# One mask product ahead of each group of attention scores, in a kernel of two transformer blocks

## The chip, the cores and the metric

The kernel runs on one core of a Trainium2 chip. The metric is the device time of one execution in microseconds. TensorE (PE) multiplies and writes to PSUM; VectorE (DVE) and ScalarE (ACT) read PSUM and do the elementwise work; GpSimd (POOL) does a few small operations; SyncE (SP) issues the weight transfers.

## The reference

The input is 256 positions of width 1024. Two blocks follow each other. The first has a causal softmax attention with a forgetting term (8 heads of 64), a retention branch, an output projection and an MLP, all modulated by a small vector c. The second applies a sparse attention (8 heads of 64 in two key groups) with pooling, an MLP, gated linear attention and another MLP, with layer norms between. For the change only the scores and their mask matter. First attention:

```python
logits = einsum(q, k) * scale
logits = logits + cum[:, :, s0:s1, None] - cum[:, :, None, :s1]
logits = where(q_pos >= k_pos, logits, -inf)
p = softmax(logits)
```

The second attention has three branches. The compressed branch scores 15 summary keys. The selected and the window branch see, at 256 positions (16 selected blocks are more than there are, and the window is 512), all keys up to the query, so each is a causal softmax over the same q with its own keys and values:

```python
s_s = einsum(q, k_sel);  p_s = masked_softmax(s_s, kpos <= t)
s_w = einsum(q, k_w);    p_w = masked_softmax(s_w, wmask)
o = gates[0] * o_c + gates[1] * o_s + gates[2] * o_w
```

## The kernel before

All matrices with weights are streamed. SyncE fetches tiles of 128 x 1024 fp32 into 6 slots, ScalarE rounds each to its high part (`whi`, L581) and VectorE takes the low part (`wlo`, L1107), and PE multiplies in three products, high by high, high by low and low by high (`three`, L1766 to L1768 and L1906 to L1908). Each engine runs a program in an order written out by hand. Semaphores are counted up by one engine and waited for by another.

Both attentions are woven into the projections around them. The dictionaries `between` name, behind which weight tile, which steps of the attention PE does. A step `S_(n)` computes the scores of group n, `T_(n)` transposes its probabilities, `V_(n)` multiplies them with the values. The groups (`GRP`, `GROUPS`) are the same in three branches: the first attention (n = 0 to 5), the selected branch (6 to 11) and the window branch (12 to 17). In each, two groups hold four heads of the first query tile (t = 0, 128 keys each) and four groups hold two heads of the second (t = 1, 256 keys each). Either way a group fills one PSUM bank of 512 fp32 columns.

`softmax_scores(n)` issues the scores. It first waits until ScalarE has taken the exponentials of the group that had the same bank (`at_exp`). Then for each head it multiplies q (stationary, 128 queries wide) with k (streamed, `kw` = 128 or 256 columns), in fp32 (L1989), which the trace shows as two passes with a weight load each. In the first attention q and k have 104 rows (64 of the head, and rows that carry the forgetting sums); in the second they have 64. Behind each head's product stands the mask product (L1990): the identity as stationary operand, `negb` streamed, both bf16 128 x 128. `negb` is 0 where a key is allowed and -1e30 where it lies ahead of the query. It is added to the head's last 128 columns, the diagonal block. Both are cast once, at the start (L725, L726). The last mask product of the group counts `at_mm` up.

Then VectorE takes each head's maximum (`maxima`, L1339), ScalarE the exponentials with their sums (`exps`, L804), VectorE in the second attention scales them by gate over sum (`weigh`, L1571 to L1575, counts `at_w`). `prob_transposes` (L2002) waits for these, VectorE copies the result out (L1347), and the values follow (L2094, L2304, L2308). The compressed branch's own scores (`cmp_scores`, L2252) are 64-row products of 15 columns, right behind `S_(6)`. The pooling products (L2321, L2322, L2330) stand between groups 11, 12 and 13.

As this kernel uses PSUM, a product with `start=True` opens a bank: it overwrites where it writes, and a product with `start=False` adds where something has been written since the bank was opened and overwrites elsewhere. The MLP (`up`) relies on this already: it opens the bank with the first product only and writes the other half with `start=False`.

Of the kernel before, what the change touches and what calls it, by code (L numbers as in the profile page):

```python
# [12 lines left out]
P = 128  # L13
# [155 lines left out]
def block_program(nc, dram, out):  # L169
    with ExitStack() as ctx:  # L170
        def sb(name, shape, dt=F32):
            return ctx.enter_context(nc.sbuf_tensor(name, shape, dt))
# [12 lines left out]
        rows = sb("rows", [P, 2, D])  # L185
        proj = sb("proj", [P, NT, 3072])
        qT = sb("qT", [P, 2 * D])
        kT = sb("kT", [P, 2 * D])
# [7 lines left out]
        identb = sb("identb", [P, P], BF16)  # L196
        negb = sb("negb", [P, P], BF16)
# [26 lines left out]
        AT = ctx.enter_context(nc.psum_tensor("AT", [P, 4, 512], F32))  # L224
# [58 lines left out]
        def bank(pb, t):  # L283

            if pb == 2:
                return AT[:, 2 + t, :]
            return PJ[:, 2 * (1 - pb if pb < 2 else pb % 2) + t, :]
# [25 lines left out]
        S_BANK = [0, 1, 0, 1, 0, 1] + [1] * 12  # L313
# [1433 lines left out]
        def _(pe):  # L1747
            mm = nc.tensor.matmul
# [21 lines left out]
            def tile_part(o, s, t, hi, lo, k0, n=512, start=False, stop=False):  # L1770

                for kk in range(KPT):
                    w = slice(512 * kk, 512 * kk + n)
                    ins = three(o[:, 0:n], hi[:, k0 + kk, rows_of(t)], lo[:, k0 + kk, rows_of(t)], whi[:, s % SPL, w],
                                wlo[:, s % SPL, w], start and kk == 0, stop and kk == KPT - 1)
                return ins
# [199 lines left out]
            def softmax_scores(n):  # L1976

                br, t, heads = GROUPS[n]
                fox = n < NF
                before = [g for g in range(0 if fox else NF, n) if S_BANK[g] == S_BANK[n]]  # L1980
                if before:
                    pe.wait_ge(at_exp, before[-1] + 1)
                kw = P * (t + 1)
                for u, h in enumerate(heads):
                    rows = slice(0, 104) if fox else slice(0, 64)
                    q = qT[rows, h * S + t * P:h * S + (t + 1) * P]
                    k0 = h * S if fox else (1024, 1536)[br] + S * (h // 4)
                    o = AT[:, S_BANK[n], u * kw:(u + 1) * kw]
                    mm(o, q, kT[rows, k0:k0 + kw], start=True, stop=False)  # L1989
                    ins = mm(o[:, kw - P:kw], identb[:, :], negb[:, :], start=False, stop=True)  # L1990
                ins.then_inc(at_mm, 1)

            def prob_transposes(n):
# [79 lines left out]
            def fox_scores(n):  # L2073
                if n == 2:
                    pe.wait_ge(hd_done, 8)
                if n == 0:
                    pe.wait_ge(hd_done, 4)
                    pe.wait_ge(cum_done, 2)
                    pe.wait_ge(ld_sel, 32)
                    pe.wait_ge(cast_done, 3)  # L2080
                softmax_scores(n)
# [87 lines left out]
            for q in range(4):  # L2169
                pe.wait_ge(xn_done, q // 2 + 1)  # L2170
                for c in range(4):
                    ins = nc.tensor.transpose(PJ[:, q, c * P:(c + 1) * P], from_proj(q // 2, 4 * (q % 2) + c), ident)
                ins.then_inc(xt_tr, 1)
            mod_sums(0)
            for s, (b, i) in enumerate(FIRST):
                for t in range(NT):
# [6 lines left out]
                    ins = tile_part(bank(b, t), T_IN + s, t, hT_hi, hT_lo, KPT * i, 512, i == 0, i == BLK - 1)  # L2183
# [97 lines left out]
            def nsa_scores(n):  # L2281
                if n == NF:
                    pe.wait_ge(nt_done, 7)
                softmax_scores(n)
# [215 lines left out]
```

## Time and profile before

| | |
|---|---|
| median of 3 runs | 1027.58 us (1026.83 to 1028.77) |
| profiled execution | 1029.0 us, of which the span is 1027.2 us |
| PE busy | 966.0 us, 94% of the span |
| VectorE, ScalarE busy | 657.4 us, 485.8 us |
| mean granted clock of PE | 0.984 |
| DMA, mean | 182 GB/s |

Times in the rows are microseconds from the start of the span, unless marked ns. PE's matmul records overlap, since products are pipelined: the distance between two starts tells what a product costs the stream behind it, its own length also contains its way through the array. PEld is the weight load, which usually runs beside the product before it. "x2" joins neighbouring instructions of one line. PEclk is the clock granted to PE as a share of 2.4 GHz. The first attention's scores lie between 84 and 117 us, the second's between 422 and 500 us; the MLPs are the long stretches between.

### The profile page before, as it was taken

The page shows a single profiled execution, that of the slowest core. Times are in us where ns is not written, and L with a number is a line of the kernel's source. Part 1 is how long each engine was busy: PE and PEld are TensorE (multiplying, and loading weights), DVE is VectorE, ACT ScalarE, POOL GpSimd, SP SyncE. Part 2 cuts the span into 40 slices and gives each one's busy share as a digit, 9 for nine tenths or more (in the row PEclk, how much of TensorE's full clock was granted, in tenths as well). Part 3 has the DMA queues.
Part 4 walks back from the last instruction along what each step waited for, and adds up shares of the span by engine and source line. Part 5 has one row for each costly group of instructions (what it writes and reads, how often), then busy time and mean ns, then how long its engine had stood idle before and what let it go on. Part 6 is the DMA issues. An engine that isn't in the chain of part 4 may idle for free.

```text
span 1027.2 us, 14930 instructions
## 1 busy us (share of the span) xinstructions
PE 966.0 (94%) x5602; PEld 824.2 (80%) x5602; DVE 657.4 (64%) x828; ACT 485.8 (47%) x734; POOL 54.0 (5%) x59
## 2 busy tenths in 40 slices
PE   3889989799999999999989999998999989999996
PEld 3768867599999987866679999996786779999995
DVE  5777897885455666555876546548545786555555
ACT  5457657454454444333345445443645725544440
POOL 3030101100000001000020000001000010000000
PEclk9999989999999999899999999999999999999998
DMA  9999776686655666411447655663542357456531
GB/s 281 297 240 290 206 210 230 234 272 206 205 178 172 209 232 159 124 41 43 143 131 237 201 199 163 196 206 106 181 150 84 118 170 263 167 187 203 183 123 41
DMA packets 109991, 186.94 MB, mean 182 GB/s; under 512 B 8696, under 2 KB 67088, under 8 KB 109920
## 3 DMA queue, kind: packets, MB, share of 16 engines
q1 hardware_dynamic: 104800, 177.33, 53.8%
q0 software_dynamic: 2592, 8.53, 3.0%
q8 instruction: 34, 0.56, 0.2%
q10 hardware_dynamic: 2544, 0.35, 0.2%
q14 instruction: 21, 0.17, 0.0%
HBM read 185.13 MB, written 1.05 MB: 181 GB/s over the span
## 4 chain that ended last, share of the span: by engine, by line
PE 81%; DVE 8%; ACT 4%; issue 3%; DMA 2%; POOL 2%; SPq 0%; POOLq 0%; ACTq 0%; DVEq 0%
PE PJ L1766 14%; PE PJ L1767 14%; PE PJ L1768 14%; PE AT L1908 8%; PE AT L1907 8%; PE AT L1906 8%; PE AT L1989 2%; POOL rstd L467 2%; DVE wlo L1107 1%; PE AT L2002 1%; PE AT L1757 1%; DMA raw<-in_w_out_dram 1%; PE AT L2033 1%; DMA raw<-in_w_in_dram 1%; DVE bn L1192 1%
## 5 line engine op out<-in xcount | busy, mean ns | idle before, releaser
L1107 DVE TENSOR_TENSOR wlo<-raw,whi 128x1024 fp32r<-128x1024 f32 x144 | 172.9, 1222 | 53.0 <-ACT whi L581 52.5
L1906 PE MATMUL AT<-hT_hi,whi 128*128 128x256 f32 x720 | 203.8, 283 | 0.0
L1908 PE MATMUL AT<-hT_hi,wlo 128*128 128x256 f32 x720 | 203.8, 283 | 0.0
L1907 PE MATMUL AT<-hT_lo,whi 128*128 128x256 f32 x720 | 203.7, 283 | 0.0
L1235 DVE TENSOR_TENSOR wlo<-raw,whi 128x1024 fp32r<-128x1024 f32 x144 | 169.9, 1222 | 32.2 <-ACT whi L639 31.6
L1766 PE MATMUL PJ<-whi,uhi 128*128 128x512 f32 x432 | 170.9, 396 | 1.5 <-DVE wlo L1107 0.9
L581 ACT ACTIVATE whi<-raw 128x1024 fp32r<-128x1024 f32 x144 | 146.9, 1055 | 48.7 <-DMA raw<-in_w_in_dram 28.5
L1767 PE MATMUL PJ<-wlo,uhi 128*128 128x512 f32 x432 | 169.4, 392 | 0.0
L1768 PE MATMUL PJ<-whi,ulo 128*128 128x512 f32 x432 | 168.7, 391 | 0.0
L639 ACT ACTIVATE whi<-raw 128x1024 fp32r<-128x1024 f32 x144 | 144.5, 1051 | 47.6 <-PE PJ L1768 43.7
L1766 PE MATMUL PJ<-whi,hT_hi 128*128 128x512 f32 (+1 forms) x320 | 133.0, 416 | 11.4 <-DVE hT_lo L1283 7.3
L1907 PEld LDWEIGHTS AT<-hT_lo,whi 128*128 128x128 f32 x720 | 138.0, 192 | 1.7
L1906 PEld LDWEIGHTS AT<-hT_hi,whi 128*128 128x128 f32 x720 | 138.0, 192 | 1.6
L1908 PEld LDWEIGHTS AT<-hT_hi,wlo 128*128 128x128 f32 x720 | 138.0, 192 | 0.0
L1244 DVE TENSOR_TENSOR pr<-pr 128x512 f32<-128x512 f32 x45 | 31.1, 692 | 161.6 <-ACT pr L649 161.6
L1768 PE MATMUL PJ<-whi,hT_lo 128*128 128x512 f32 (+1 forms) x320 | 126.0, 394 | 0.0
L1767 PE MATMUL PJ<-wlo,hT_hi 128*128 128x512 f32 (+1 forms) x320 | 125.9, 393 | 0.0
L649 ACT ACTIVATE pr<-AT 128x512 f32<-128x512 f32 x45 | 26.9, 598 | 190.3 <-PE AT L1908 190.3
L1766 PEld LDWEIGHTS PJ<-whi,uhi 128*128 128x128 f32 x432 | 81.6, 189 | 18.8 <-issue 1.9
L1768 PEld LDWEIGHTS PJ<-whi,ulo 128*128 128x128 f32 x432 | 81.5, 189 | 17.5
L1767 PEld LDWEIGHTS PJ<-wlo,uhi 128*128 128x128 f32 x432 | 81.7, 189 | 15.3 <-issue 0.2
L1766 PEld LDWEIGHTS PJ<-whi,hT_hi 128*128 128x128 f32 x320 | 62.2, 194 | 29.2 <-DVE hT_lo L1283 8.7
(310 smaller groups left out, 1079.5 us busy)
## 6 DMA issues: line engine op xcount, KB each, us to landing
raw<-in_mlp_w_dram SPq DMA_DIRECT2D x128, 512.0 KB, 4.8
raw<-in_w_in_dram SPq DMA_DIRECT2D x32, 512.0 KB, 6.1
raw<-in_w_ada_dram SPq DMA_DIRECT2D x32, 512.0 KB, 5.1
raw<-in_w_mlp_in_dram SPq DMA_DIRECT2D x32, 512.0 KB, 4.9
raw<-in_w_mlp_out_dram SPq DMA_DIRECT2D x32, 512.0 KB, 5.0
raw<-in_c_w_in_dram SPq DMA_DIRECT2D x24, 512.0 KB, 4.5
raw<-in_w_ada_dram SPq DMA_DIRECT2D x32, 256.0 KB, 5.9
raw<-in_a_w_in_dram SPq DMA_DIRECT2D x12, 512.0 KB, 5.4
```

Of the source, the lines that this page charges most:

```text
L581: nc.scalar.activation(whi[:, s % SPL, :], raw_slot(r), ACT.Copy).then_inc(hi_done, 1)
L639: nc.scalar.activation(whi[:, s % SPL, :], raw_slot(r), ACT.Copy).then_inc(hi_done, 1)
L649: nc.scalar.activation(pr[:, 0, :], AT[:, j % 2, :], ACT.Relu).then_inc(relu_done, 1)
L1107: tt(wlo[:, n % SPL, :], raw_slot(r), whi[:, n % SPL, :].bitcast(F32), ALU.subtract).then_inc(raw_done, 1)
L1235: tt(wlo[:, s % SPL, :], raw_slot(r), whi[:, s % SPL, :].bitcast(F32), ALU.subtract)\
L1244: tt(pr[:, 1, :], pr[:, 0, :], pr[:, 0, :], ALU.mult).then_inc(usq, 1)
L1766: mm(o, a, hi, start=start, stop=False)
L1767: mm(o, a, lo, start=False, stop=False)
L1768: return mm(o, b, hi, start=False, stop=stop)
L1906: mm(o, whi[:, s % SPL, c], hT_hi[:, k, :], start=first, stop=False, skip_group_check=True)
L1907: mm(o, whi[:, s % SPL, c], hT_lo[:, k, :], start=False, stop=False, skip_group_check=True)
L1908: ins = mm(o, wlo[:, s % SPL, c], hT_hi[:, k, :], start=False, stop=last, skip_group_check=True)
```

## The change

The mask product moves from behind each head's scores to the head of the group, and there is one for all heads. Its output is the last 128 of each head's `kw` columns: for t = 0 the whole bank, for t = 1 two runs of 128 columns with 128 between them. Its streamed operand is `negb`, repeated for each head by a stride of zero. It opens the bank (`start=True`). The score products then have `start=False`: they add to the mask in the diagonal blocks and overwrite in the first 128 columns of t = 1. The last score product of the group counts `at_mm` up.

```diff
--- before.py
+++ after.py
@@ -1981,13 +1981,15 @@
                 if before:
                     pe.wait_ge(at_exp, before[-1] + 1)
                 kw = P * (t + 1)
+                n_heads = len(heads)
+                mm(AT[:, S_BANK[n], :].rearrange("p (u k) -> p u k", u=n_heads)[:, :, kw - P:kw], identb[:, :],
+                   negb[:, :].unsqueeze(1).broadcast_to([P, n_heads, P]), start=True, stop=False, skip_group_check=True)
                 for u, h in enumerate(heads):
                     rows = slice(0, 104) if fox else slice(0, 64)
                     q = qT[rows, h * S + t * P:h * S + (t + 1) * P]
                     k0 = h * S if fox else (1024, 1536)[br] + S * (h // 4)
                     o = AT[:, S_BANK[n], u * kw:(u + 1) * kw]
-                    mm(o, q, kT[rows, k0:k0 + kw], start=True, stop=False)
-                    ins = mm(o[:, kw - P:kw], identb[:, :], negb[:, :], start=False, stop=True)
+                    ins = mm(o, q, kT[rows, k0:k0 + kw], start=False, stop=True, skip_group_check=True)
                 ins.then_inc(at_mm, 1)
 
             def prob_transposes(n):
```

## Rows read from the trace of the kernel before

**Rows 1.** The page, chain that ended last: share of the span by engine.

```profile
PE 81%; DVE 8%; ACT 4%; issue 3%; DMA 2%; POOL 2%; SPq 0%; POOLq 0%; ACTq 0%; DVEq 0%
```

**Rows 2.** Windows: start:end us, length, busy us of each engine (instructions), PEclk, DMA share, GB/s.

```profile
458.00:468.00 10.00, 10.00 (x63) 7.38 (x62) 7.13 (x14) 6.00 (x14) 0.00 (x0) 1.00 0.33 105
...
500.00:512.00 12.00, 9.57 (x60) 6.90 (x60) 10.96 (x19) 5.40 (x9) 0.00 (x0) 1.00 0.55 175
...
535.00:600.00 65.00, 64.93 (x412) 58.98 (x412) 40.49 (x40) 33.49 (x39) 0.00 (x0) 1.00 0.63 207
```

**Rows 3.** The score products, PE: ns min/median/max, first and last start, forms.

```profile
L1989 PE MATMUL AT<-kT,qT x96: 272/376/579, 84.4 to 498.7; 64*128 64x128 f32 x32, 64*128 64x256 f32 x32, 104*128 104x128 f32 x16, 104*128 104x256 f32 x16
```

**Rows 4.** PE timeline, four heads, 104 rows: start us, us, engine, line, operands, count [idle <-releaser].

```profile
84.67 0.22 PE L1990 MATMUL AT<-negb,identb 128*128 128x128 bf16 x1
84.73 0.44 PE L1989 MATMUL AT<-kT,qT 104*128 104x128 f32 x2
85.00 0.22 PE L1990 MATMUL AT<-negb,identb 128*128 128x128 bf16 x1
```

**Rows 5.** PE timeline, two heads, 104 rows, first group on the chain.

```profile
95.54 0.60 PE L1989 MATMUL AT<-kT,qT 104*128 104x256 f32 x2
95.98 0.22 PE L1990 MATMUL AT<-negb,identb 128*128 128x128 bf16 x1
...
96.55 0.47 PE L1766 MATMUL PJ<-whi,hT_hi 128*128 128x512 f32 x1
```

**Rows 6.** Timeline of PE's weight loads (PEld), compressed branch's scores, 64 rows.

```profile
425.17 2.42 PEld L2252 LDWEIGHTS AT<-sc,qT 64*128 64x128 f32 x21
```

**Rows 7.** PE timeline, four heads, 64 rows, full clock.

```profile
467.53 0.48 PE L1989 MATMUL AT<-kT,qT 64*128 64x128 f32 x2
467.95 0.23 PE L1990 MATMUL AT<-negb,identb 128*128 128x128 bf16 x1
468.11 0.48 PE L1989 MATMUL AT<-kT,qT 64*128 64x128 f32 x2
...
469.75 1.95 PE L2330 MATMUL PJ<-proj,acc 128*128 128x256 f32 x8
```

**Rows 8.** PE timeline: first group of the second attention, and the one at the lower clock.

```profile
422.86 0.48 PE L1989 MATMUL AT<-kT,qT 64*128 64x128 f32 x2
...
425.17 4.80 PE L2252 MATMUL AT<-sc,qT 64*128 64x15 f32 x32
...
433.00 0.79 PE L1989 MATMUL AT<-kT,qT 64*128 64x128 f32 x2
...
436.61 0.78 PE L1766 MATMUL PJ<-whi,hT_hi 128*128 128x512 f32 x1
```

**Rows 9.** PE timeline, two heads, 64 rows.

```profile
462.10 0.70 PE L1989 MATMUL AT<-kT,qT 64*128 64x256 f32 x2
...
463.58 0.65 PE L2321 MATMUL PJ<-tab,proj 128*128 128x256 f32 x2
```

**Rows 10.** The chain in order of time, ahead of the transposes at 95 us.

```profile
79.64 8.16 DMA raw<-in_w_in_dram
```

**Rows 11.** Timeline, waits of the probabilities' transposes, and the weighting before one.

```profile
95.08 0.63 PE L2002 MATMUL AT<-cst,pr 128*128 128x128 f32 x4 [0.63 <-ACT kT L785]
...
471.74 0.69 DVE L1575 TENSOR_TENSOR pr<-pr,rinv 128x512 f32<-128x512 f32 x1
...
472.54 0.63 PE L2002 MATMUL AT<-cst,pr 128*128 128x128 f32 x4 [0.25 <-issue]
...
501.85 0.63 PE L2002 MATMUL AT<-cst,pr 128*128 128x128 f32 x4 [0.58 <-issue]
```

**Rows 12.** Windows, columns as in rows 2: the clock around the second attention.

```profile
433.00:437.00 4.00, 4.00 (x14) 2.76 (x14) 1.97 (x7) 0.94 (x3) 0.00 (x0) 0.50 0.42 131
475.30:478.90 3.60, 3.60 (x11) 2.82 (x11) 2.40 (x6) 1.51 (x8) 0.00 (x0) 0.53 0.00 0
...
422.00:441.30 19.30, 19.30 (x87) 15.90 (x86) 8.92 (x21) 5.44 (x22) 0.00 (x0) 0.65 0.26 82
```

## The prediction

> **What bounds the kernel now.** I read the page's chain of waits first: TensorE (PE) holds 81% of it, so time taken out of PE counts where nothing else is late [rows 1]. The windows then say where that holds. From 458 to 468 us, inside the second attention, PE is busy for the whole 10 us, VectorE for 7.13, ScalarE for 6.00 and the DMA engines for a third; from 535 to 600 us, in the MLP that follows, PE has 64.93 of 65 us. From 500 to 512 us PE has only 9.57 of 12 and VectorE 10.96 [rows 2]. The profiled execution took 1029.0 us, 1027.2 of them span; the median of the runs is 1027.58. I make the sum in the profile's own microseconds and take it off the median.
>
> **What the change removes and adds.** There are 18 groups of scores with 48 pairs of a head and a query tile: 16 in the first attention, with 104 rows, and 32 in the second, with 64 rows. Each pair ends in a mask product of its own, 48 in all. The change puts one mask product ahead of each group: 512 columns for the 6 groups of four heads (t = 0), 256 for the 12 groups of two (t = 1). The columns streamed stay the same, 48 x 128 = 6 x 512 + 12 x 256. What can change is what stands between the streams, so I price those gaps in the PE timeline; its "x2" is one fp32 product of two passes, 0.27 to 0.58 us long each as recorded, overlapping [rows 3].
>
> *104 rows, t = 0.* A mask starts at 84.67, the next pair at 84.73, its mask at 85.00 [rows 4]: 0.33 a head. Two passes alone are 0.22 (a pass with its load hidden is 0.11, as in rows 6) and the mask's stream is 0.06; the 0.05 left over is a 0.11 us load of q that so short a mask can't hide. Afterwards only the group's head has a mask, 0.22 long, and it covers that load. A group goes from 4 x 0.335 = 1.34 to 0.22 + 8 x 0.112 = 1.11, saving 0.23. There are two.
> *104 rows, t = 1.* The pair at 95.54 takes 0.44 up to its mask at 95.98; the group ends where the next stream is listed at 96.55 [rows 5]. The same 0.055 goes at each of two masks: 0.11 a group, four groups, 0.45.
>
> *64 rows, t = 0.* Pair to mask is 0.42 (467.53 to 467.95), mask to next pair 0.16 (to 468.11): 0.58 a head, against 0.33 with 104 rows and the same columns [rows 4, 7]. The pair is 0.20 longer, the mask 0.10. I read this as the price of alternating a 64-row product with a 128-row one: 0.10 until the old stream is out and 0.11 for a load that isn't hidden, on the way in, and somewhat less on the way back. The nearest row for 64 rows behind 64 rows are the compressed branch's scores: 21 loads in 2.42 us, the last of them 0.19 long, each with a short stream behind it, so 2.23 / 20 = 0.112 a pass, with other weights each time [rows 6]. With the masks gone from between, a pass should cost that. The group from 467.53 to 469.75 takes 2.22, with the edges on both sides 2.37. Afterwards: mask 0.22, way in 0.21, eight passes 0.90, way out 0.20, together 1.53. **Saved 0.84**, and 0.80 in the like group at 473.1, whose successor waits a little anyway. The group from 422.86 to 425.17 is followed by 64-row products, so its way out goes too: 1.19. The fourth, 433.00 to 436.61, runs at the lower level of the clock, 1.2 GHz (granted 0.50) [rows 8, 12]: 3.61 and edges of 0.5, against mask 0.43, eight passes of 0.213 (twice a stream of 0.107) and edges of 0.8, 2.95 in all; 1.15. Sum for t = 0: 3.98.
> *64 rows, t = 1.* 462.10 to 463.58, with the edges 1.63 [rows 9]; afterwards mask 0.11, way in 0.21, four passes of 0.216, way out 0.20, 1.38. Saved 0.25, eight groups: 2.0.
>
> **What of it lies on the path.** The savings of the two groups of rows 4 lie beside other work. The transposes at 95.08 wait for ScalarE's last head transposes, PE idle for 0.63 us [rows 11], and the chain leads from these to a weight transfer listed from 79.64, 8.16 us long [rows 10]. Scores that end 0.46 earlier only lengthen that wait: cost 0; if the cover were gone, 0.46 more gain. Behind it PE is never idle in the four t = 1 groups: 0.45.
> In the second attention the chain to ask after is the softmax: maxima, exponentials, weighting, then the transposes of the probabilities. It counts from the end of the scores, and what PE does between that end and the transposes stays. It is exposed at 472.54 (PE idle 0.25; VectorE's weighting runs from 471.74 for 0.69) and at 501.85 (0.58) [rows 11]. The group's last instruction will be a score pass instead of a mask. A mask's record is 0.23 long [rows 7] and PE streams on 0.12 behind its start: it completes 0.11 after PE has gone on. A score pass of 128 columns is 0.27 long [rows 3] and PE goes on 0.31 behind its start (0.11 stream, 0.20 way out): it completes 0.04 before. So the softmax chain starts 0.15 earlier against PE, 0.3 over the two waits. No wait is added, and the mask stands behind the semaphores that the first score stands behind now. VectorE's stretch from 500 to 512 hangs on the last scores and moves forward whole; so does the MLP behind it [rows 2].
> Sum: 3.98 + 2.0 + 0.45 + 0.3 = 6.7 to 6.8 us. **Forecast 1027.6 - 6.8 = 1020.8 us.** Bounds of the gaps: from below only the unhidden 0.055 of rows 4 per head, 40 heads on the path, 2.2; from above 0.31 for each of 20 alternations avoided (32 less 12), 6.2, with the lower clock's extra, the way out at 425, the 0.45 and the waits 7.5. I take the value of rows 6 and 7, the nearest. Below nothing is excluded for the gaps, since columns and waits stay; only the new form of output (a rival below) could take back more than 2.2.
>
> **Rivals.**
> *Clock, upward.* From 475.3 to 478.9 the granted clock is 0.53, so some 3.4 us ran at 1.2 GHz; before it PE did short pieces, the four 64-row heads of the group at 473.1 among them. From 422 to 441.3 it is 0.65, 13.5 us at the lower level, behind the compressed scores [rows 12]. Denser groups leave fewer gaps ahead of both. If the later stretch goes, 1.7 us more come back: 1019.1; if the long one is shorter by as much too, 1017.4. Against it: the small products around the scores stay.
> *Own price.* A 64-row pass of 128 or 256 columns exposes its load behind another head's too. Then only the mask's 0.16 goes: 4 x (0.64 - 0.22) + 8 x (0.32 - 0.11) + 0.45 = 3.8, so 1023.8. Rows 6 speak against it, though their passes have 15 columns. The Trainium skill, TensorEngine Tiling (Array Packing), section Key Properties, says that changing the tiling mode drains the engine; by that rule one way in and one way out stay for each group, and not this rival.
> *Split output.* For t = 1 the new mask writes two separated runs of 128 columns, and every new mask reads its operand two or four times over; no row here shows a product that does. If those of t = 1 cost twice their 0.11, 12 x 0.11 = 1.3 goes: 1022.1; if three times, 1023.4. The Trainium skill, PSUM — Partial Sum Buffer, section Specifications, says that a non-contiguous pattern slows products significantly; by it this would be the result.
> *Given back before VectorE.* The groups from 462 to 475 are close together, and the 2.7 us from their last score to the end of the weighting (469.75 to 472.43) may become the pace. Each slot holds 2.5 us or more of other PE work, so this takes 1 us at most: 1021.8; it is in the forecast's own spread.
> *Slower.* With the scores shorter, PE meets the waits between 441 and 515 us with fewer columns per microsecond, and the clock stays at 1.2 GHz. Half of every low microsecond is lost, so 13.6 us more of it than now cancel the 6.8, and 18 more give 1029.8. That is the long stretch of today a second time, in a place where PE is busy throughout [rows 2]; little speaks for it.
>
> **How the numbers follow.** Forecast with the clock as now 0.52; clock upward 0.24; split output 0.08; own price 0.07; nothing measurable 0.04; slower 0.05. The forecast's own spread is 1 us either side. The range 1017.2 to 1024.0 takes in clock upward, split output and most of own price; outside stay nothing, slower, and tails of some 0.08. Within 0.2%, 2.1 us, is about what a measurement can't tell from no change; faster means below 1025.5, which all cases but the last two give: 0.90; same 0.05; slower 0.05.
>
> **What would show it.** L1990 has 18 products instead of 48. In a 64-row group pairs follow each other at 0.22 (t = 0) and 0.43 (t = 1); if they stand at 0.4 and 0.6, own price is right. From the mask at 467 to the product behind the group 1.5 us, where 2.37 stand now. The 256-column masks take 0.11 until the next load starts to wait for them, or the split output is right. PE's idle before the transposes at 95 us grows by some 0.4. The granted clock between 470 and 480 tells of the clock rival. Wrong altogether is the prediction if the groups shrink as said and the span doesn't: then a wait downstream that I took for one anchored on PE is not.

## The result, and the profile after

The changed kernel took 1014.66 us (median of 4 runs, 1013.91 to 1015.31) against 1027.20 for the one before, run beside it. The ratio is 0.9881 with a 95% interval of 0.9862 to 0.9899. By the ratio 12.2 us come off, by the medians 12.5, where 6.8 were forecast; the time is below the range. On another chip later the same kernel gave a ratio of 0.9924 (0.9895 to 0.9953). The profiled execution took 1015.01 us, 1013.2 of them span: 14.0 less span than before.

In the chain that ended last PE has 78% where it had 81% [rows 1]. The page's row after:

```profile
PE 78%; DVE 9%; ACT 4%; issue 3%; DMA 2%; POOL 2%; SPq 0%; POOLq 0%; ACTq 0%; DVEq 0%
```

The mask products by line, with durations in ns (min/median/max), first and last start and forms. There are 18 for the 48 of before:

```profile
L1985 PE MATMUL AT<-negb,identb x18: 272/273/650, 84.0 to 485.6; 128*128 128x256 bf16 x12, 128*128 128x512 bf16 x6
```

PE's timeline after: a group of four heads and one of two in the first attention (they answer to [rows 4, 5]), then the second attention's first group and the one that ran at the lower clock (both [rows 8]), a group of two [rows 9], one of four [rows 7], and two waits that are new, at 435.06 and 465.64.

```profile
83.98 0.39 PE L1985 MATMUL AT<-negb,identb 128*128 128x512 bf16 x1
84.20 1.05 PE L1992 MATMUL AT<-kT,qT 104*128 104x128 f32 x8
85.09 1.04 PE L2071 MATMUL AT<-cst,proj 128*64 128x128 f32 x8
...
94.55 0.63 PE L2004 MATMUL AT<-cst,pr 128*128 128x128 f32 x4 [0.95 <-ACT kT L785]
95.01 0.27 PE L1985 MATMUL AT<-negb,identb 128*128 128x256 bf16 x1
95.12 1.03 PE L1992 MATMUL AT<-kT,qT 104*128 104x256 f32 x4
95.80 0.58 PE L1766 MATMUL PJ<-whi,hT_hi 128*128 128x512 f32 x1
96.22 0.40 PE L1767 MATMUL PJ<-wlo,hT_hi 128*128 128x512 f32 x1
...
421.77 0.28 PE L1768 MATMUL PJ<-whi,hT_lo 128*128 128x280 f32 x1
421.90 0.39 PE L1985 MATMUL AT<-negb,identb 128*128 128x512 bf16 x1
422.22 1.16 PE L1992 MATMUL AT<-kT,qT 64*128 64x128 f32 x8
423.21 3.64 PE L2254 MATMUL AT<-sc,qT 64*128 64x15 f32 x32
...
429.61 0.65 PE L1985 MATMUL AT<-negb,identb 128*128 128x512 bf16 x1
430.19 1.24 PE L1992 MATMUL AT<-kT,qT 64*128 64x128 f32 x8
431.36 0.50 PE L1766 MATMUL PJ<-whi,hT_hi 128*128 128x512 f32 x1
...
435.06 0.28 PE L1985 MATMUL AT<-negb,identb 128*128 128x256 bf16 x1 [0.23 <-ACT pr L804]
...
454.27 0.27 PE L1985 MATMUL AT<-negb,identb 128*128 128x256 bf16 x1
454.47 1.13 PE L1992 MATMUL AT<-kT,qT 64*128 64x256 f32 x4
455.53 0.70 PE L2323 MATMUL PJ<-tab,proj 128*128 128x256 f32 x2
...
459.43 0.38 PE L1985 MATMUL AT<-negb,identb 128*128 128x512 bf16 x1
459.74 1.16 PE L1992 MATMUL AT<-kT,qT 64*128 64x128 f32 x8
460.83 1.99 PE L2332 MATMUL PJ<-proj,acc 128*128 128x256 f32 x8
...
465.64 0.50 PE L1766 MATMUL PJ<-whi,uhi 128*128 128x512 f32 x1 [0.19 <-DVE ulo L1587]
...
489.52 0.63 PE L2004 MATMUL AT<-cst,pr 128*128 128x128 f32 x4 [0.44 <-issue]
```

Four starts of the kernel before, for cuts and distances that its rows ahead of the prediction don't hold:

```profile
96.86 0.39 PE L1767 MATMUL PJ<-wlo,hT_hi 128*128 128x512 f32 x1
...
421.13 0.40 PE L1766 MATMUL PJ<-whi,hT_hi 128*128 128x280 f32 x1
...
422.64 0.28 PE L1768 MATMUL PJ<-whi,hT_lo 128*128 128x280 f32 x1
...
499.04 0.48 PE L1766 MATMUL PJ<-whi,hT_hi 128*128 128x512 f32 x1
```

The groups in 64 rows shrank as the working said. From mask to the product behind, the four-head group takes 1.40 us (459.43 to 460.83) where 2.22 stood, the two-head group 1.26 (454.27 to 455.53) where 1.48 stood. Neither explains 14 us. The windows do. First the stretches of the kernel before (start:end, length, busy us of PE, PEld, DVE, ACT, POOL, then PEclk, DMA share, GB/s):

```profile
420.00:445.00 25.00, 25.00 (x118) 20.05 (x117) 12.10 (x25) 7.67 (x26) 0.00 (x0) 0.73 0.25 81
445.00:500.00 55.00, 54.07 (x287) 37.00 (x287) 31.80 (x67) 21.35 (x63) 0.00 (x0) 0.97 0.20 63
500.00:530.00 30.00, 23.78 (x143) 19.18 (x143) 24.61 (x41) 9.96 (x16) 6.62 (x10) 0.94 0.45 135
```

and the same of the kernel after:

```profile
420.00:445.00 25.00, 24.09 (x136) 19.37 (x137) 15.16 (x35) 10.53 (x35) 0.00 (x0) 0.93 0.26 90
445.00:500.00 55.00, 52.41 (x303) 37.92 (x302) 38.82 (x75) 23.20 (x60) 0.00 (x0) 1.00 0.30 94
500.00:530.00 30.00, 26.13 (x175) 23.18 (x174) 24.74 (x34) 14.36 (x19) 6.60 (x10) 1.00 0.56 165
```

A granted clock of 0.73 over 25 us means that 2 x 0.27 x 25 = 13.5 us of it ran at 1.2 GHz and the rest at 2.4; after it is 3.5. From 500 to 530 the 0.94 of before is 3.6 us, after it is none; between 445 and 500 another 3.3 went. So 17 us less ran at the lower level. Located slice by slice, the lower level lay at 427.6 (13.7 us long), 475.4 (3.4) and 523.2 (3.4) before, and at 427.0 (3.4) alone after; a stretch at 140 us and one at the end are in both.

To put this on the path I cut the execution at the same products of PE in both traces. Stage A goes from the weight block ahead of group 6 to the first product behind group 7 (421.13 to 436.61 before), B from there to the first product behind group 17 (499.04), C over the next hundred products (the layer norm), D to PE's last product. In brackets is how much of the stage ran at 1.2 GHz, all in us:

| stage | before | after | less | of it clock | of it gaps and waits |
|---|---|---|---|---|---|
| start to A | 421.13 | 420.25 | 0.88 | 0 | 0.88 |
| A | 15.48 [9.0] | 11.10 [3.4] | 4.38 | 2.8 | 1.6 |
| B | 62.43 [8.1] | 55.47 [0] | 6.96 | 3.6 | 3.4 |
| C | 23.60 | 23.47 | 0.13 | 0 | 0.13 |
| D | 495.21 [3.4] | 493.58 [0] | 1.63 | 1.6 | 0 |

The clock's share in A is half of the time no longer spent at the lower level. In D half of 3.4 would be 1.7, of which D shows 1.63. For B it is taken from two executions shown below, in which B ran at full clock and still had the old order (58.73 in the kernel before, run once more, and 58.98 with groups 6 and 7 alone changed). In all some 8.0 us come from the clock and 6.0 from the gaps, with 0.88 ahead of A in the latter, of which the forecast had worked out 0.45; the first attention's length differs by more than that between executions of one kernel, so the rest is not assigned. The gaps are what was forecast; the clock is what was not.

Two names return in the expectations. "Density" says that the products of groups 6 and 7 and what lies between them decide the long stretch at the lower clock. "Phase" says that it hangs on the moment at which the pieces happen to lie.

### The profile page after: what moved, and what is told of

It is laid out like the page before. It is cut to its first block, busy times and chain, and to the rows that moved or that the text cites. A ratio compares the mean times of both kernels' runs of the same rounds, so it can differ in the third digit from the quotient of the medians.

```text
span 1013.2 us, 14870 instructions
## 1 busy us (share of the span) xinstructions
PE 951.8 (94%) x5572; PEld 816.1 (81%) x5572; DVE 656.6 (65%) x828; ACT 485.2 (48%) x734; POOL 53.9 (5%) x59
## 4 chain that ended last, share of the span: by engine, by line
PE 78%; DVE 9%; ACT 4%; issue 3%; DMA 2%; POOL 2%; SPq 0%; POOLq 0%; ACTq 0%; DVEq 0%
PE PJ L1766 14%; PE PJ L1767 13%; PE PJ L1768 13%; PE AT L1908 9%; PE AT L1907 9%; PE AT L1906 9%; DVE wlo L1107 2%; POOL rstd L467 2%; PE AT L1992 1%; DMA raw<-in_w_out_dram 1%; PE AT L2035 1%; PE AT L1757 1%; DMA raw<-in_w_in_dram 1%; DVE bn L1192 1%; DVE acc L1130 1%
```

## The experiments

**First question: are the gaps an alternation of 64 and 128 rows, and does the clock hang on groups 6 and 7?** Two kernels widen the second attention's scores from 64 to 96 rows, one with the old order and one with the new. The rows that q gets in addition are zero, so the scores stay the same. GpSimd clears them early, and PE waits for that once:

```diff
+            pool.wait_ge(tr_done, units(3))
+            nc.gpsimd.memset(qT[64:96, :], 0.0).then_inc(q_zero, 1)
...
-                    rows = slice(0, 104) if fox else slice(0, 64)
+                    rows = slice(0, 104) if fox else slice(0, 96)
...
+                    pe.wait_ge(q_zero, 1)     # ahead of group 6
```

The old order in 96 rows:

> The kernel before, with one edit: the second attention's q and k products take 96 rows instead of 64 (rows 64 to 95 of q are zeroed once by GpSimd during the first MLP, so the scores are the same). The mask stays behind every head. Theory 'alternation': what cost 0.58 and 0.79 us a head was going between a 64-row and a 128-row product, and 96 rows count as 128. So a head falls to 0.33 (t = 0) and 0.49 (t = 1), as with 104 rows in the first attention: 16 x 0.25 + 16 x 0.30 = 8.8 us without any change of the clock, so at most 1018.5, and some 7 us less if the low stretches of the clock go too as they did in the changed kernel: 1011.5. Rival 'own price' (a 64-row fp32 product is slow by itself, or the mask behind each head is what costs): a head stays at 0.42 to 0.63 for the pair plus the mask, 1025 or more.

Measured: 1014.87 us against 1027.71, ratio 0.9888 (0.9847 to 0.9929), as much as the change itself, with every mask product still behind its head. The rival "own price" had 1025 or more. Stage B is 53.53 us, and the lower stretch near 427 is 3.4 long. PE's timeline of this kernel, the four-head group:

```profile
458.10 0.39 PE L2000 MATMUL AT<-kT,qT 96*128 96x128 f32 x2
458.32 0.22 PE L2001 MATMUL AT<-negb,identb 128*128 128x128 bf16 x1
458.38 0.44 PE L2000 MATMUL AT<-kT,qT 96*128 96x128 f32 x2
458.66 0.22 PE L2001 MATMUL AT<-negb,identb 128*128 128x128 bf16 x1
```

From pair to pair it is 0.28 to 0.34 us, where 64 rows took 0.58 [rows 7]; mask to the next pair is 0.06, where 64 rows took 0.16. The columns are the same and so is the order; only the rows differ. So the 0.24 us a head comes with the 64 rows. That a 64-row product isn't slow by itself shows in the changed kernel, where its passes follow each other at 0.111 (worked out below). What is left is the price of going from 128 rows to 64 and back, and the two together show it. The Trainium skill, TensorEngine Tiling (Array Packing), section Key Properties, says that the engine drains when its tiling mode changes; the 0.58 against 0.34 agrees with that.

The new order in 96 rows:

> The changed kernel, with the second attention's q and k products at 96 rows (as in row96_old). Theory 'alternation': the 12 groups lose the one way in and way out that is left to each, 0.31 us, less where the successor has 64 rows itself: 11 x 0.31 = 3.4 us under the changed kernel's 1014.7, 1011.2; the groups at 459 and 464 us take 0.22 + 0.90 with nothing between. Rival 'own price': no gain, 1014.7. Should this be right it beats both kernels.

Measured: 1014.10 us, ratio 0.9877 (0.9836 to 0.9917). The time is that of the change, within the interval, and the 1011.2 that was expected is missed; but stage B is 52.51 us against 55.47, 2.96 less for its ten groups. From the product ahead of a group to the third start behind it, a group of four heads takes 1.65 us where 64 rows take 2.04, and most groups of two take 1.55 where 64 rows take 1.94. So one way in and one way out, which the new order still pays per group, are 0.39. Two of the ten groups gain nothing, since PE waits there: group 8 for the exponentials of group 7, and group 13 for VectorE, with 2.33 in 96 rows and 2.34 in 64. The profiled execution gave 3.0 us back in D (496.61 with 10.2 us at the lower level, 493.58 without any after the change).

Then the change for groups 6 and 7 alone, and for all but these:

```diff
+                new = n in (6, 7)          # the other kernel: n not in (6, 7)
...
+                if new:
                     mm(AT[:, S_BANK[n], :].rearrange("p (u k) -> p u k", u=n_heads)[:, :, kw - P:kw], identb[:, :],
...
+                    else:
+                        mm(o, q, kT[rows, k0:k0 + kw], start=True, stop=False)
+                        ins = mm(o[:, kw - P:kw], identb[:, :], negb[:, :], start=False, stop=True)
```

> The kernel before, with the new order of mask and scores in groups 6 and 7 alone (the first two of the second attention, from 422 us on). Gaps: 1.2 + 1.2 = 2.3 us. Theory 'density': the clock's long low stretch (13.7 us from 427.6) came of these two groups and the 32 small products between them; it shrinks to 3.4 us as in the changed kernel, 5 us more, so 1020; the later stretches at 475 and 523 us stay. Rival 'phase': whether a stretch falls low depends on when its pieces happen to lie, and the stretch may stay: 1025.

> The changed kernel, with the old order in groups 6 and 7 alone (the complement of only67). Theory 'density': the long low stretch from about 427 us is back and only it: 2.3 + 5 us over the changed kernel, 1022; the stretches at 475 and 523 us are gone as in the changed kernel. Rival 'phase': the long stretch is not back, 1017.

Measured: 1022.10 us for groups 6 and 7 alone, ratio 0.9941 (0.9921 to 0.9961), and 1021.87 for the others alone, 0.9957 (0.9937 to 0.9978). Windows of the first, around groups 6 and 7 and over the rest of the attention:

```profile
420.00:445.00 25.00, 24.20 (x143) 19.01 (x142) 14.49 (x30) 10.45 (x32) 0.00 (x0) 0.93 0.31 101
445.00:500.00 55.00, 53.76 (x302) 37.49 (x302) 36.27 (x74) 23.62 (x63) 0.00 (x0) 1.00 0.24 75
```

and of the second:

```profile
420.00:445.00 25.00, 25.00 (x118) 20.10 (x117) 12.44 (x28) 8.19 (x29) 0.00 (x0) 0.73 0.23 81
445.00:500.00 55.00, 53.58 (x305) 38.40 (x305) 36.28 (x75) 25.61 (x67) 0.00 (x0) 1.00 0.23 72
```

In these profiles two groups of the eighteen bring the clock of the first window from 0.73 to 0.93, all of what the full change brings, and the other sixteen bring nothing to it. Stage A is 11.10 us with groups 6 and 7 alone, exactly the length after the full change, and 15.20 without them. Stage B with the old order at full clock is 58.98, so the ten groups in it save 58.98 - 55.47 = 3.5. The stretches at 475 and 523 are gone in both kernels, though the expectation for groups 6 and 7 alone had them stay; that one has two others instead, at 708 and 831, and came out at 1022.10 where 1020 was expected. No one part of the change is needed for 475 to go, and the kernel with the first attention alone changed (below) hasn't got it either.

**Second question: one of the two, or both, and does the place in time matter?** The switch was set to `n == 6` and to `n == 7`:

> The kernel before, new order in group 6 alone (422 us). Gap 1.1 us. The long low stretch (13.7 us from 427.6 in the kernel before; 3.4 us in the run with groups 6 and 7 new; 13.7 us again with both old) either needs group 7's denser scores to end, then it stays about as long, 10 us or more, 1026; or it was the earlier end of the 32 small products behind group 6 that let it end, then 3.4 us are left, 1022 ('phase').

> The kernel before, new order in group 7 alone (433 us). Gap 1.2 us. If group 7's density is what ends the stretch ('density'), it falls from 13.7 to 10 us or less, as group 7 begins 5 us into it: 1024 to 1025. If only the shift of the small products counts ('phase'), it stays 13.7 us and the time is 1026.5.

Measured: 1023.24 us against 1026.43, ratio 0.9970 (0.9951 to 0.9990), and 1024.39, ratio 0.9974 (0.9953 to 0.9995). The lower level around 428 lasted 10.2 us in both profiles, between the 13.7 of neither and the 3.4 of both; the window's clock is 0.80 in each. Group 6 alone, then group 7 alone:

```profile
420.00:445.00 25.00, 25.00 (x132) 19.54 (x129) 14.38 (x30) 9.29 (x30) 0.00 (x0) 0.80 0.23 83
```

```profile
420.00:445.00 25.00, 25.00 (x128) 20.51 (x126) 13.61 (x31) 9.67 (x30) 0.00 (x0) 0.80 0.26 85
```

The old order alone gave 6.8 us in two other executions (below), so one execution of each tells one new group from both, but not from none. How the two groups share the effect isn't shown: group 7 comes after the clock has fallen, and in one execution of the changed kernel (the second of the third question) the clock had risen again at 429.4, just before group 7 began at 429.45.

Then sixteen transposes into a bank that is overwritten afterwards were put ahead of group 6, some 2 us of dense work that only moves everything behind it, once with the old order and once with the new:

```diff
+                if f == 6:
+                    for _ in range(4):
+                        for c, a in enumerate(srcs):
+                            nc.tensor.transpose(AT[0:64, 2 + f % 2, c * P:(c + 1) * P], a, ident)
```

> The kernel before, with 16 more transposes (the last four query transposes of the second attention four times over, same data to the same place) ahead of group 6: PE busy 2.0 us longer there, everything behind it 2.0 us later. The order of mask and scores is the old one. 'Density' alone: the long stretch of 13.7 us stays whatever the shift, 1029.7. 'Phase': its length changes with the shift, to 7 or 3.4 us or less, and the time comes out under 1028.

> The changed kernel with the same 16 transposes ahead of group 6, 2.0 us more. 'Density': the low stretch behind group 6 stays 3.4 us or goes, 1016.7. 'Phase': a shift can bring 7 us or more of it back, 1018.5 or more.

Measured: 1031.27 us with the old order, ratio 1.0029 (1.0012 to 1.0045), and 1019.81 with the new, 0.9934 (0.9908 to 0.9960). The window of the old order with the shift, then that of the new:

```profile
420.00:445.00 25.00, 25.00 (x118) 21.00 (x115) 10.40 (x23) 7.03 (x24) 0.00 (x0) 0.66 0.21 74
```

```profile
420.00:445.00 25.00, 24.55 (x142) 20.50 (x140) 14.15 (x30) 9.65 (x30) 0.00 (x0) 0.86 0.24 82
```

The shift's own work is in both times. The lower level lasted 17.1 us with the old order and 6.8 with the new: 3.4 more in each than in the recorded profile without the shift, and 10.3 between the two orders in either place. Neither is what "density" alone had (13.7 and 3.4); the new order came out as "phase" had said, and the old moved the other way, longer instead of shorter. With one profile of each, where the scores fall in time seems to matter, but it doesn't undo the difference between the orders. The old order with the shift is the rival Slower in small: a stretch 3.4 us longer, and a time above that of before. Stage B with the new order is again short, 55.29.

**Third question: how much of this is one execution's luck?** Each kernel was run unedited twice more with a profile and nothing else.

> The kernel before, unedited, one more profile. 'Density': with groups 6 and 7 old, the stretch at 1.2 GHz that begins near 427 us is 6.8 to 17.1 us long, as in the four profiles that had them old. 'Phase' alone: it can as well be 3.4 us.

> The kernel before, unedited, a second more profile: 6.8 us or more at 1.2 GHz near 427 us by 'density', 3.4 us as likely by 'phase' alone.

> The changed kernel, unedited, one more profile. 'Density': the stretch near 427 us is 3.4 us, at most 6.8. 'Phase' alone: 10 us or more is as likely as with the kernel before.

> The changed kernel, unedited, a second more profile: the stretch near 427 us 3.4 us, at most 6.8, by 'density'; 10 us or more as likely by 'phase' alone.

Measured, one execution each: 1024.41 and 1029.39 us for the kernel before (a third beside them took 1029.02), 1015.77 and 1017.85 for the one after. The first execution of the kernel before, windows:

```profile
420.00:445.00 25.00, 24.32 (x129) 19.18 (x127) 13.00 (x28) 8.66 (x29) 0.00 (x0) 0.86 0.22 70
445.00:500.00 55.00, 53.90 (x300) 37.03 (x298) 35.01 (x73) 23.76 (x64) 0.00 (x0) 1.00 0.23 75
500.00:530.00 30.00, 24.55 (x159) 21.63 (x159) 22.85 (x35) 8.50 (x13) 6.60 (x10) 0.94 0.47 148
```

The second execution of the kernel after:

```profile
420.00:445.00 25.00, 23.77 (x135) 19.29 (x135) 14.97 (x35) 10.22 (x34) 0.00 (x0) 0.93 0.26 85
445.00:500.00 55.00, 52.43 (x303) 37.91 (x302) 38.85 (x75) 23.01 (x60) 0.00 (x0) 1.00 0.30 95
500.00:530.00 30.00, 26.18 (x164) 23.40 (x163) 23.45 (x33) 13.44 (x19) 6.60 (x10) 0.94 0.48 147
```

The same kernel before had the long stretch at 426 only 6.8 us long this time and none at 475. Its span is 4.6 us shorter: 4.5 in A and B, 1.6 ahead of A, and 1.5 given back in D to stretches at 518, 699 and 832. Its second execution has the stretches of the recorded profile, 13.7, 3.4 and 3.4 us. The kernel after, with its short stretch unchanged, had one at 511 and two more at 692 and 825, each 3.4 us, which the recorded profile doesn't have: D is 496.60 against 493.58. All profiles together, by the lower stretch near 427:

| order of groups 6 and 7 | profiles | length near 427, us | stage A, us |
|---|---|---|---|
| both old | 6 | 13.7 (four), 6.8 (two) | 14.65 to 15.48 |
| one new | 2 | 10.2 (both) | 12.37 (group 6), 13.93 (group 7) |
| both new | 5 | 3.4 (all) | 11.10 to 11.13 |
| 96 rows, old or new order | 3 | 3.4 (all) | 10.36 to 11.14 |

The two shifted kernels are left out here; "both old" holds the kernel before three times, the one with the other sixteen groups changed, and the two kernels of the next question. The shortest A of the six with the old order is 3.5 us longer than the longest of the five with the new (14.65 against 11.13), and some 2 of that are gaps; that much is the change's own. The stretches at 508 to 523, 689 to 708 and 822 to 835 come and go with either order. In D one of them adds 1.4 to 1.6 us, three together 3.0 to 3.1. The one at 475 comes and goes with the old order: it is in two of the three profiles of the kernel before, and in none with only the first attention changed, which has the old groups in the second. B is 61.09 there against 62.43, so it costs 1.3. It is in none of the five with groups 6 and 7 new; whether it can come there isn't shown.

**Fourth question: what are the single parts worth, and does it hold on another chip?** The switch was set to `fox` (the first attention's six groups), and to the second attention's eight groups of two heads:

```diff
+                new = fox                  # the other kernel: n >= NF and t == 1
```

> The kernel before, new order in the first attention's six groups alone (104 rows, 84 to 112 us). The prediction's terms: the two groups of four heads save 0.23 each and PE's wait before the transposes at 95 us eats it; the four groups of two heads save 0.11 each, 0.45 us in all: 1026 to 1027.5, not to be told from the kernel before. The clock's stretches from 427 us on stay as they are. Rival: with the waits at 95 us eating more, nothing at all is left.

> The kernel before, new order in the eight groups of two heads of the second attention alone (n = 8 to 11 and 14 to 17, from 442 us on). Gaps: 8 x 0.25 = 2.0 us. Theory 'density' (only groups 6 and 7, around the 32 small products, decide the long low stretch): it stays 13.7 us or thereabouts, so 1025. Rival: any denser group lifts the clock, then under 1022.

Measured: 1026.52 us against 1026.64, ratio 0.9993 (0.9975 to 1.0010), and 1024.78, ratio 0.9989 (0.9971 to 1.0007). The first attention's share is below what can be told, as 0.45 us had to be. The eight groups' ratio is inconclusive too, but their trace has stage B at full clock, 56.65 us against the 58.98 with the same groups in the old order: 2.33. From the product ahead to the third start behind, seven of the eight give 0.25 to 0.27 each; the eighth gives 0.46, since with groups 6 and 7 alone changed PE waits there as well. In this profile the lower stretch near 427 was 6.8 us long with groups 6 and 7 in the old order, the second such execution beside the one above; A is 14.73. The expectation had it stay at about 13.7. So 6.8 is in reach of the old order, and in 64 rows 3.4 has been seen with both groups new alone.

Last, the kernel after and the one with 96 rows and the new order, unedited, on that chip:

> The changed kernel once more, unedited, to see how far its executions spread on this chip beside row96_new_b: 1014 to 1016.

> row96_new once more. Its profile showed the two parts of the second attention 3.3 us shorter than the changed kernel's (10.77 against 11.10, and 52.51 against 55.47 us), yet three more stretches of 3.4 us at 1.2 GHz elsewhere (508, 689, 822 us). If these are chance, more executions show it 2 to 3 us under the changed kernel; if its shorter attention moves what follows into them every time, it stays within 1 us.

Measured: 1017.74 us for the kernel after (6 runs, 1014.73 to 1023.02), ratio 0.9924 (0.9895 to 0.9953), and 1013.72 with 96 rows (6 runs, 1012.61 to 1015.43), ratio 0.9871 (0.9851 to 0.9891). The kernel after was expected at 1014 to 1016. The 96-row kernel beats both it and the kernel before on this chip. Its B is 52.18 against 55.33 and its A 10.36 against 11.11, 3.9 us. The medians lie 4.0 apart, but the two profiled executions only 0.7: the one of the kernel after was the fastest of its six (1014.73), and the one of the 96-row kernel had more at the lower level elsewhere (10.2 us at 17, 6.8 at 201, 3.4 at 508). So the 3.9 is what the attention gives; how much of it a single execution keeps differs. Its window around groups 6 and 7 has the clock that the new order has in 64 rows:

```profile
420.00:445.00 25.00, 24.32 (x150) 20.93 (x148) 16.07 (x36) 11.44 (x36) 0.00 (x0) 0.93 0.32 105
```

## Why the prediction was wrong in size, and where it was right

- **What bounds it: right.** PE had the path; where it got shorter the span did, except ahead of 95 us.
- **Four heads in 64 rows (t = 0), 3.98: the full-clock terms right.** 467.53 to 469.75 became 459.43 to 460.83, 0.82 for the 0.84 named. Group 6 went from 2.53 (422.64, where the product ahead starts, to 425.17) to 1.44 (421.77 to 423.21), 1.09; to the third start behind it is 2.77 and 1.58, the 1.19 of the working. A pass behind a pass costs (460.83 - 459.74 - 0.20) / 8 = 0.111 us, 0.112 were named. Group 7 has 1.75 from mask to the product behind it (429.61 to 431.36), since the clock rose while it ran; the working had it at the lower clock throughout and at 2.95 with its edges. The like group at 473.09 gave 0.6 for 0.80: it takes 2.93 with the old order at full clock, from the product ahead to the third start behind, and 2.34 after, since PE now waits for VectorE at 465.64.
- **Two heads in 64 rows (t = 1), 2.0: right.** 1.48 became 1.26 between listed starts. From the product ahead to the third start behind, seven of the eight groups gave 0.25 to 0.27 each; group 8 lost 0.14, by the wait at 435.06.
- **First attention, 0.45 on the path and 0.46 lost in a wait: the groups right, the rest not shown.** The group from 83.98 takes 1.11 to the product at 85.09, as worked out. The idle time of PE ahead of the transposes is 0.95 where 0.63 stood [rows 11], but that tells nothing: it is 0.42, 0.63 and 1.08 in the three profiles of the kernel before, and none, 0.59, 0.92 and 0.95 in the four of the kernel after. In the group at 95 us the distance up to the second product behind fell from 1.32 (95.54 to 96.86) to 1.21 (95.01 to 96.22), the 0.11 of the working. What the path gained can't be told from none: stage A begins at 419.55 to 421.57 before and at 419.76 to 421.37 after.
- **Softmax chain, 0.3: the two waits right, "no wait is added" wrong.** The wait of 0.25 at 472.54 is gone, that of 0.58 at 501.85 became 0.44 at 489.52: 0.39 together. Two waits came. At 435.06 the mask of group 8 stands 0.23 us for ScalarE's exponentials of group 7. The semaphore is the old one, but the groups now start 5.45 us apart (429.61 to 435.06), where 9.1 lay between them. At 465.64 PE waits 0.19 for VectorE's low part of the next operand. Together they take back the 0.39.
- **Given back before VectorE: came in small, inside the forecast's spread.** The wait at 465.64 lies between the groups that the rival named. It costs the 0.2 us by which the group of 473.09 fell short, and in 96 rows that group gains nothing more.
- **Own price, Split output: neither came, and both had small chances.** Passes are 0.111 apart at a new head too. The 256-column mask in two runs takes 0.11 from its start to the next pass (95.01 to 95.12), half of what the 512-column mask in one run takes (0.22, 83.98 to 84.20). The Trainium skill, PSUM — Partial Sum Buffer, section Specifications (TRN2), has a non-contiguous pattern slow products significantly; two runs of 128 columns in one bank show nothing of it.
- **The failed step: the forecast "with the clock as now", and the cap of 1.7 + 1.7 us in the rival Clock, upward.** The rival named both stretches and the denser groups, but let the long one shrink by as much as the short one "as well", 3.4 us of 13.5. It shrank by 10.3, worth some 5 us between these two executions and still (6.8 - 3.4) / 2 = 1.7 between the closest two of all; and a third stretch, at 523, is missing after, worth 1.6. The long one is what the change did; that 475 and 523 were missing too in the recorded profile was luck as far as the runs show. With 6.0 of gaps and 8.0 of clock the sum is the 14.0 between the spans. Nothing in the rows supported the cap: with the whole long stretch at stake, half of its 13.5 us, the case reached to 1027.6 - 6.8 - 1.7 - 6.7 = 1012.4, and the measured time lies inside that.

What was overlooked stood in [rows 8, 12]: from group 6 to the end of group 7 it is 13.75 us (422.86 to 436.61), 9.0 of them at the lower clock, and the edit touches the work just ahead of the long stretch and inside it. That groups 6 and 7 together make the difference is shown: 6.8 us or more in all six profiles with both old, 3.4 in all five with both new, and 3.4 with the old order too once the rows are 96. Why it is these isn't shown: in the 96-row kernels the columns are the same and the gaps shorter, but so is the time that all of it takes. The stretches at 475, 508 to 523, 689 to 708 and 822 to 835 stay open; nothing here starts or stops them at will.

## What to carry to other kernels

Where scores or other products of 64 rows stand between 128-row ones, count the switches and not only the columns: fill the rows up to 96 with zeros if the operand's rows are free, or else put all products of one height side by side. Then look for the wait that becomes the pace: in 96 rows two of the ten groups of stage B gained nothing for that reason. When an edit makes PE denser next to a stretch at the lower clock, price that stretch's whole length both ways before fixing a range. And compare clock stretches over several executions of either kernel: of the 14.0 us between the two recorded profiles some 3 came from two stretches that one unedited kernel has in some executions and not in others: 1.3 at 475, in two of three profiles of the kernel before, and 1.6 at 523, at 518 in the third.

## What the runs showed of the hardware

- A 64-row product that alternates with a 128-row one costs 0.24 us for the way there and back: 0.58 us a head of 128 columns, 0.34 in 96 rows with the same columns. Of this 0.14 lies between pair and mask (0.42 against 0.28) and 0.10 behind the mask (0.16 against 0.06). Around a whole group of 64-row products it is 0.39 us (2.04 against 1.65, 1.94 against 1.55), and in 96 rows it is gone.
- A product that writes two separated runs of 128 columns and reads its streamed operand with a stride of zero costs what its columns cost: 0.11 us for 256 bf16 columns (95.01 to 95.12), 0.22 for 512 in one run (83.98 to 84.20).
- The same kernel, unedited, has its stretches at 1.2 GHz in different places and lengths from one execution to the next: 1022.8 to 1029.5 us over 24 runs of the kernel before on one chip, and a stretch of 13.7 us in two of its profiles and of 6.8 in the third. With two microseconds of dense transposes ahead it was 3.4 us longer than in the recorded profile of either order, in one profile each.
- The clock can fall to 1.2 GHz while PE's records leave no idle time: from 420 to 445 us of the kernel before, PE is busy 25.00 of 25.00 us at a mean granted clock of 0.73.
